# MoE expert weights of a two-block transformer kernel: one transfer per expert with both halves of a row, in place of one transfer per half over all eight experts

## The chip, the cores and the metric

The kernel runs on one core of a Trainium2 chip. The metric is the device time of one execution in microseconds (us), lower is better. The core has a matrix engine (PE, with its weight loads PEld), a vector engine (DVE), a scalar engine (ACT), a sync engine (SP, here the only one that issues transfers) and 16 DMA engines that move data from HBM into on-chip memory.

## The reference

Two transformer blocks in float32 on 256 tokens of width 1024. The change touches one stage of the first block, a mixture of experts: each token is processed by two of eight experts, whose weights are the largest arrays of the program.

```
D_MODEL = 1024; SEQ = 256; N_EXPERTS = 8; TOP_K = 2; FFN_EXPERT = 3584
...
top_logits, top_idx = lax.top_k(logits, TOP_K)
gates = jax.nn.softmax(top_logits, axis=-1)
...
def expert_block(args):
    xb, e = args
    h = jax.nn.silu(xb @ w1[e]) * (xb @ w3[e])     # w1, w3: 1024 x 3584 for each expert
    return h @ w2[e]                               # w2: 3584 x 1024 for each expert
```

Around it stand, in this order, two mixer layers (gated delta rule, convolution, attention), a dense SwiGLU between them, and, after the experts, a second block with two attention layers and two gated feed-forward layers. None of these is touched.

## The kernel before

**Storage.** The host lays the expert weights out as `ws_moe`: for each of the 8 experts 42 slots, and a slot is 128 rows (one for each partition) of 2048 floats, so a row is 8 KB, a slot 1 MB, and the same slot of the next expert lies 42 slots (44 MB) further on. In the first 28 slots of an expert a row holds for one column block of 128 the w1 weights of all eight input blocks and then the w3 weights of the same (4 KB each: the two "halves", h = 0 and 1). In the last 14 slots a row holds weights of w2.

**Chunks.** The stage runs over 84 chunks (`CHUNKS`), each of 4 MB: 4 input blocks (`CK = 4`) of 128 x 256 weights for all eight experts. 56 chunks belong to the up phases (w1 and w3), 28 to the down phases (w2). Chunks are loaded in turn into two buffers, `mring[0]` (traced as ring) and `mring[1]` (traced as arena), whose order in a partition is expert, half, 512 floats. Two chunks, one in each buffer, are called a cycle below.

**Who waits for what.** SP issues the loads of chunk c once `chunk_over(c - 2)` holds (L385-392, called at L444): PE has done the products that read chunk c - 2 directly, and DVE and ACT have copied out of it what the dynamic row blocks need. In before each chunk is two transfers (L452), one for each half, and both count up `moe_w0` or `moe_w1`. PE (L904), ACT (L1337) and DVE (L1848) start on a chunk when all of its transfers have landed. DVE then copies with L1860 and ACT with L1351 the weights of the experts that own the dynamic row blocks into small buffers (`CB`, three in turn), and PE multiplies at L913: for each of a chunk's four input blocks 24 row blocks of 32 rows, of which the first eight read the chunk itself and the others the copies. L1833 and L1838/L1840 take the sums out of the accumulators, L894 transposes hidden rows.

**Streams outside the stage.** All other weights come through L416 (`slot_dma`) as 1 MB tiles whose 128 rows of 8 KB are contiguous in HBM.

Of the kernel before, what the change touches and what calls it, by code (L numbers as in the profile page):

```python
# [7 lines left out]
P = 128  # L8
# [9 lines left out]
KD = D // P  # L18
# [6 lines left out]
NE = 8  # L25
FE = 3584
KE = FE // P
# [6 lines left out]
SLOT = 16  # L34
# [10 lines left out]
PK = 4  # L45
NPART = KE // PK
CK = 4
# [60 lines left out]
PHASES = moe_phases()  # L108
PH_CHUNKS = [KD // CK if i < PK else PK // CK for _, i in PHASES]
CHUNKS = [(ph, st) for ph, n in enumerate(PH_CHUNKS) for st in range(n)]  # L110
# [10 lines left out]
def up_index(ph):  # L121

    part, i = PHASES[ph]
    return PK * part + i


def flips_first(c):
# [32 lines left out]
def build(nc, ws_a, ws_moe, ws_b, xT, ctxT, cT, pvec, prow, wsmall, wrouter, cst_d, out):  # L160
    with ExitStack() as ctx:
        sems = {}

        def sem(name):
            if name not in sems:
                sems[name] = ctx.enter_context(nc.semaphore(name))
            return sems[name]
# [157 lines left out]
        SELT = arena_at(17408, NG * T).rearrange("p (g t) -> p g t", g=NG)  # L325
        IOTA2 = arena_at(18944, NROW)
        ws_up = ws_moe.rearrange("(e s) p (w c) -> s w p e c", e=NE, w=2)
        ws_dn = ws_moe.rearrange("(e s) p c -> s p e c", e=NE)
        HT = Mf[:, 0:5 * NROW].rearrange("p (q r) -> p q r", q=5)

# [82 lines left out]
        @block.sync  # L413
        def _(sp):
            def slot_dma(pos, src):
                return sp.dma_start(ring[:, pos * SLOT * P:(pos + 1) * SLOT * P], src)  # L416

            def stream(n):
                if n >= RING:

                    name, count = FREE[n - RING]
                    sp.wait_ge(sem(name), count)
                array, i = SOURCE[n]
                slot_dma(n % RING, (ws_a if array == "a" else ws_b)[i]).then_inc(sem(f"weights{n % RING}"), 16)

            sp.dma_start(X[:, 1], xT).then_inc(sem("x_in"), 16)
            sp.dma_start(cst[:, :], cst_d).then_inc(sem("consts_in"), 16)
            sp.dma_start(pv[:, :], pvec).then_inc(sem("params_in"), 16)
            sp.dma_start(pr[:, :, :], prow).then_inc(sem("rows_in"), 16)
            sp.dma_start(wsm[:, :, :, :], wsmall).then_inc(sem("small_in"), 16)  # L430
            sp.dma_start(wrt[:, :, :], wrouter).then_inc(sem("router_in"), 16)
            sp.dma_start(cvec[:, :, :], cT).then_inc(sem("c_in"), 16)
            for n in range(SLOT0["moe"]):
                stream(n)
            sp.wait_ge(sem("tile_done"), TILE["out1"] + 8)
            sp.wait_ge(sem("ada_done"), 16)
            for c in range(NCH):
                ph, st = CHUNKS[c]
                part, i = PHASES[ph]
                if c == 1:  # L440
                    sp.wait_ge(sem("x_even"), 12)
                    sp.wait_ge(sem("x_odd"), 12)
                if c >= 2:
                    chunk_over(sp, c - 2)  # L444
                to = mring[c % 2].rearrange("p (e h c) -> p e h c", e=NE, h=2)
                for h in range(2):
                    if i < PK:
                        src = ws_up[up_index(ph), h, :, :, st * CK * P:(st + 1) * CK * P]
                    else:
                        t = (2 * (i - PK) + h) * KE + PK * part  # L450
                        src = ws_dn[2 * KE * KD // SLOT + t // SLOT, :, :, t % SLOT * P:(t % SLOT + CK) * P]
                    sp.dma_start(to[:, :, h], src).then_inc(sem(f"moe_w{c % 2}"), 16)  # L452

            for n in range(SLOT0["moe"], len(SOURCE)):
                i = n - SLOT0["moe"]
                if i < RING:
                    if n % RING < 4:
                        chunk_over(sp, NCH - 2)
                    else:
                        unit_over(sp, (CK * NCH - 1) // 3 * 3)  # L460
                    slot_dma(n % RING, ws_b[SOURCE[n][1]]).then_inc(sem(f"weights{n % RING}"), 16)
                    if i == RING - 1:
                        sp.wait_ge(sem("combined"), KD)
                        sp.dma_start(X[:, 0], ctxT).then_inc(sem("ctx_in"), 16)
                else:
                    stream(n)
            for t in range(TT):
                sp.wait_ge(sem("out_ready"), t + 1)
                sp.dma_start(out[t * P:(t + 1) * P, :], Yf[:, t * D:(t + 1) * D]).then_inc(sem("stored"), 16)
            sp.wait_ge(sem("stored"), 16 * TT)  # L470
# [3 lines left out]
        def _(pe):  # L474
# [169 lines left out]
            for l in range(2):  # L644
# [140 lines left out]
                for g in range(G):  # L785
                    r = g % 2 * HD
                    for i in range(2):
                        c = i * HD
# [60 lines left out]
                else:  # L849
# [48 lines left out]
                    for c in range(NCH):  # L898
# [2 lines left out]
                        last = ends_phase(c)  # L901
                        if flips_first(c):
                            flip(up_index(ph - 1))
                        pe.wait_ge(sem(f"moe_w{c % 2}"), 32 * (c // 2 + 1))  # L904
                        if i >= PK:
                            pe.wait_ge(sem("hidden_stored"), 2 * PK * (part + 1))

# [171 lines left out]
        def _(act):  # L1079
# [80 lines left out]
            for l in range(2):  # L1160
# [143 lines left out]
                else:  # L1304
# [27 lines left out]
                    for c in range(NCH):  # L1332
                        ph, st = CHUNKS[c]
                        ended = ends_phase(c - 1) and PHASES[ph - 1][1] < PK
                        if ended:
                            silu(ph - 1, 0)
                        act.wait_ge(sem(f"moe_w{c % 2}"), 32 * (c // 2 + 1))  # L1337
                        for kk in range(CK):
                            u = CK * c + kk
                            if kk == 2 and ended:  # L1340
# [119 lines left out]
        def _(dve):  # L1460
# [82 lines left out]
            for l in range(2):  # L1543
# [217 lines left out]
                else:  # L1761
# [81 lines left out]
                    for c in range(NCH):  # L1843
                        ph, st = CHUNKS[c]
                        ended = ends_phase(c - 1)
                        if ended:
                            take_rows(ph - 1, 0)
                        dve.wait_ge(sem(f"moe_w{c % 2}"), 32 * (c // 2 + 1))  # L1848
                        for kk in range(CK):
                            u = CK * c + kk  # L1850
                            if kk == 2 and ended:
# [316 lines left out]
```

## Time and profile before

| | us |
|---|---|
| median of 3 runs (3202.76 to 3207.5) | 3204.41 |
| the profiled execution, own time | 3191.41 |
| its span | 3189.6 |
| transfers from `ws_moe` | 168 of 2 MB, 352 MB in all |
| PE busy | 2887.9 (91% of the span) |
| DVE busy | 1565.4 (49%) |
| ACT busy | 1042.2 (33%) |

The page gives averages over stages with different limits, so it is read by stage. The expert stage fills about a third of the span, from some 770 us (first loads) and 855 us (both buffers cycling) to some 1920 us. In the page's slices it is the stretch in which the DMA digit stands at 9. A row of the windows view gives for a stretch the busy time of each engine, the granted clock of PE, the busy share of the 16 DMA engines and the GB/s moved. A row of the chain view gives start, length and what the end of the program waited for at that moment.

### The profile page before, as it was taken

The page shows a single profiled execution, that of the slowest core. Times are in us where ns is not written, and L with a number is a line of the kernel's source. Part 1 is how long each engine was busy: PE and PEld are TensorE (multiplying, and loading weights), DVE is VectorE, ACT ScalarE, POOL GpSimd, SP SyncE. Part 2 cuts the span into 40 slices and gives each one's busy share as a digit, 9 for nine tenths or more (in the row PEclk, how much of TensorE's full clock was granted, in tenths as well). Part 3 has the DMA queues.
Part 4 walks back from the last instruction along what each step waited for, and adds up shares of the span by engine and source line. Part 5 has one row for each costly group of instructions (what it writes and reads, how often), then busy time and mean ns, then how long its engine had stood idle before and what let it go on. Part 6 is the DMA issues. An engine that isn't in the chain of part 4 may idle for free.

```text
span 3189.6 us, 67930 instructions
## 1 busy us (share of the span) xinstructions
PE 2887.9 (91%) x26308; PEld 1876.5 (59%) x26308; DVE 1565.4 (49%) x5142; ACT 1042.2 (33%) x2749; POOL 0.2 (0%) x4
## 2 busy tenths in 40 slices
PE   8979999978888888888888887989999999899998
PEld 7858887856455555555555545444444444556887
DVE  5641005563567676777676673784322210454331
ACT  3121002221455545554555552253211100243210
POOL 0000000000000000000000000000000000000000
PEclk9979999988999999999999998999999999999999
DMA  5444434454599999999999981100121221211441
GB/s 206 167 172 171 146 133 158 151 207 159 191 327 322 326 321 325 327 327 315 329 318 330 322 306 65 58 26 27 66 77 69 79 79 66 79 54 54 154 150 66
DMA packets 205858, 576.06 MB, mean 181 GB/s; under 512 B 6496, under 2 KB 6624, under 8 KB 179040
## 3 DMA queue, kind: packets, MB, share of 16 engines
q1 hardware_dynamic: 205536, 571.72, 52.0%
q8 instruction: 208, 3.41, 0.4%
q14 instruction: 114, 0.93, 0.1%
HBM read 570.65 MB, written 1.05 MB: 179 GB/s over the span
## 4 chain that ended last, share of the span: by engine, by line
PE 60%; DMA 21%; DVE 13%; issue 3%; ACT 2%; DVEq 1%; SPq 1%; ACTq 0%
PE P L497 43%; DMA ring<-ws_moe 20%; PE P L913 4%; DVE arena L1860 4%; DVE ring L1860 2%; PE P L686 1%; PE P L544 1%; PE P L608 1%; DVE small L1518 1%; PE P L618 1%; DVEq L1857 1%; PE P L627 1%; PE P L881 1%; PE P L576 1%; PE P L958 1%
## 5 line engine op out<-in xcount | busy, mean ns | idle before, releaser
L497 PE MATMUL P<-arena,ring 128*128 128x256 f32 (+1 forms) x2784 | 900.2, 484 | 24.7 <-ACT arena L1157 24.7
L497 PEld LDWEIGHTS P<-arena,ring 128*128 128x128 f32 x2784 | 531.9, 192 | 383.0 <-issue 335.4
L913 PE MATMUL P<-arena 128*32 128x256 f32 x6496 | 368.4, 379 | 12.1 <-DVE rstd L1833 6.6
L913 PE MATMUL P<-ring,arena 128*32 128x256 f32 x4256 | 279.3, 414 | 80.0 <-DMA ring<-ws_moe 71.2
L497 PE MATMUL P<-X_sb,ring 128*128 128x256 f32 x1504 | 333.7, 383 | 2.9 <-ACT X_sb L1136 1.6
L497 PEld LDWEIGHTS P<-X_sb,ring 128*128 128x128 f32 x1504 | 286.6, 192 | 45.1 <-issue 3.1
L1860 DVE COPY arena<-ring 128x256 f32 x1120 | 234.6, 290 | 146.8 <-DMA ring<-ws_moe 134.6
L913 PEld LDWEIGHTS P<-arena 128*32 128x32 f32 x6496 | 213.3, 110 | 150.4 <-DVE ring L1860 9.1
L1860 DVE COPY arena<-arena 128x256 f32 x1120 | 233.7, 290 | 74.1 <-DMA arena<-ws_moe 63.3
L913 PEld LDWEIGHTS P<-ring,arena 128*32 128x32 f32 x4256 | 148.3, 119 | 196.5 <-DMA ring<-ws_moe 83.7
L1351 ACT ACTIVATE arena<-ring 128x256 f32 x560 | 181.5, 405 | 222.5 <-DMA ring<-ws_moe 163.6
L1351 ACT ACTIVATE arena<-arena 128x256 f32 x560 | 180.9, 405 | 120.7 <-PE P L913 60.5
L913 PE MATMUL P<-arena,MIX 128*32 128x256 f32 x3360 | 192.0, 379 | 14.9 <-DVE Y L1838 7.5
L2004 DVE SCALAR_TENSOR_TENSOR arena<-P,pv,arena 128x510 f32<-128x510 f32 (+1 forms) x88 | 54.2, 616 | 290.0 <-ACT arena L1399 201.4
L1916 DVE SCALAR_TENSOR_TENSOR X_sb<-P,mod,X_sb 128x256 f32<-128x256 f32 x48 | 23.2, 484 | 296.7 <-PE P L497 296.1
L913 PEld LDWEIGHTS P<-arena,MIX 128*32 128x32 f32 x3360 | 119.2, 110 | 80.6 <-DVE arena L1860 13.3
L913 PE MATMUL P<-ring,MIX 128*32 128x256 f32 x2016 | 127.5, 401 | 37.9 <-DMA ring<-ws_moe 25.0
L1860 DVE COPY ring<-ring 128x256 f32 x560 | 118.4, 290 | 65.4 <-DMA ring<-ws_moe 57.5
L497 PE MATMUL P<-MIX,ring 128*128 128x256 f32 (+1 forms) x512 | 145.7, 441 | 2.2 <-issue 2.2
L1860 DVE COPY ring<-arena 128x256 f32 x560 | 118.3, 289 | 39.6 <-DMA arena<-ws_moe 35.0
L1351 ACT ACTIVATE ring<-ring 128x256 f32 x280 | 91.8, 406 | 104.7 <-DMA ring<-ws_moe 70.2
L497 PEld LDWEIGHTS P<-MIX,ring 128*128 128x128 f32 x512 | 99.4, 195 | 44.1 <-issue 33.5
(360 smaller groups left out, 2564.7 us busy)
## 6 DMA issues: line engine op xcount, KB each, us to landing
ring<-ws_moe SPq DMA_DIRECT2D x84, 2048.0 KB, 13.8
arena<-ws_moe SPq DMA_DIRECT2D x84, 2048.0 KB, 15.5
ring<-ws_b SPq DMA_DIRECT2D x137, 1024.0 KB, 4.8
ring<-ws_a SPq DMA_DIRECT2D x67, 1024.0 KB, 4.9
cst_sb<-cst SPq DMA_DIRECT2D x1, 1664.0 KB, 8.5
X_sb<-xT SPq DMA_DIRECT2D x1, 1024.0 KB, 4.8
X_sb<-ctxT SPq DMA_DIRECT2D x1, 1024.0 KB, 4.9
out<-Y SPq DMA_DIRECT2D x2, 512.0 KB, 2.6
```

The lines of the kernel that those rows point to most:

```text
L497: ins = nc.tensor.matmul(bank(i, n), blockap(s, b % SLOT), rhs(kk), start=kk == 0, stop=kk == k - 1)
L544: ins = nc.tensor.matmul(P0[32 * j:32 * j + 32, b, 256 * half:256 * half + 256], csil[:, k, :], w, start=k == 0, stop=k == KD - 1)
L576: ins = nc.tensor.matmul(P1[:, 0, 0:n], c_("ones"), SQH[:, k, 0:n], start=k == 0, stop=k == KD - 1)
L608: nc.tensor.matmul(P1[:, (2 * p + i) % 4, 0:nk * P], q, kk, start=True, stop=True)\
L618: ins = nc.tensor.matmul(P0[i * HD:(i + 1) * HD, p % 2, 0:P], vfn(h + i, j), ptb[:, (2 * p + i) % 4, j * P:(j + 1) * P], start=j == 0, sto ...
L627: ins = nc.tensor.transpose(P0[:, 2 + i, j * P:(j + 1) * P], pb[:, (2 * p + i) % 6, j * P:(j + 1) * P], c_("ident"))
L686: ins = nc.tensor.matmul(P1[c:c + HD, 2 * i + h, r * HD:(r + 1) * HD], lhs[c:c + HD, g], cident[c:c + HD] if rhs is None else rhs[c:c + HD ...
L881: ins = nc.tensor.matmul(acc8(n % 8)[:, 0:w], XTM[:, t, k * P:(k + 1) * P], SEL[:, t, at:at + w], start=t == 0, stop=t == TT - 1)
L913: ins = nc.tensor.matmul(acc(g // 2)[BR * j:BR * (j + 1), g % 2], x[:, b * BR:(b + 1) * BR], weights_of(b), start=k == 0, stop=last and kk ...
L1351: ins = a.activation(CB[u % 3][:, NDVE + j].rearrange("p (h c) -> p h c", h=2), src, ACT.Copy)
L1860: ins = v.tensor_copy(CB[u % 3][:, j].rearrange("p (h c) -> p h c", h=2), src)
L2004: L(v.scalar_tensor_tensor(f3[:, :, 1:], b3[:, :, 0:T - 1], pv[:, w0 + 3 * m:w0 + 3 * m + 1], f3[:, :, 1:], ALU.mult, ALU.add))
```

## The change

A chunk of an up phase becomes eight transfers, one for each expert: 128 rows, and of each row two pieces of 2 KB that lie 4 KB apart (w1's and w3's). A chunk of a down phase becomes sixteen transfers, one for each expert and half: 128 rows with one piece of 2 KB. The pieces, their number and their places in the buffers are as before; the waits of PE, ACT and DVE count the new number of transfers (`landed`). The waits of SP are as before, ahead of the first transfer of a chunk.

```diff
+def landed(c):
+    return sum(16 * NE * (1 if PHASES[CHUNKS[n][0]][1] < PK else 2) for n in range(c % 2, c + 1, 2))
...
         ws_up = ws_moe.rearrange("(e s) p (w c) -> s w p e c", e=NE, w=2)
+        ws_row = ws_moe.rearrange("(e s) p (w c) -> e s p w c", e=NE, w=2)
         ws_dn = ws_moe.rearrange("(e s) p c -> s p e c", e=NE)
...
                 to = mring[c % 2].rearrange("p (e h c) -> p e h c", e=NE, h=2)
-                for h in range(2):
+                for e in range(NE):
                     if i < PK:
-                        src = ws_up[up_index(ph), h, :, :, st * CK * P:(st + 1) * CK * P]
-                    else:
+                        sp.dma_start(to[:, e], ws_row[e, up_index(ph), :, :, st * CK * P:(st + 1) * CK * P])\
+                            .then_inc(sem(f"moe_w{c % 2}"), 16)
+                        continue
+                    for h in range(2):
                         t = (2 * (i - PK) + h) * KE + PK * part
-                        src = ws_dn[2 * KE * KD // SLOT + t // SLOT, :, :, t % SLOT * P:(t % SLOT + CK) * P]
-                    sp.dma_start(to[:, :, h], src).then_inc(sem(f"moe_w{c % 2}"), 16)
+                        sp.dma_start(to[:, e, h], ws_dn[2 * KE * KD // SLOT + t // SLOT, :, e, t % SLOT * P:(t % SLOT + CK) * P])\
+                            .then_inc(sem(f"moe_w{c % 2}"), 16)
...
-                        pe.wait_ge(sem(f"moe_w{c % 2}"), 32 * (c // 2 + 1))
+                        pe.wait_ge(sem(f"moe_w{c % 2}"), landed(c))
```

The order of transfers on SP before, from the second pair of chunks of the first up phases on to the first down chunks (shape: partitions x experts x floats):

```order
43 L452 DMA ring<-ws_moe 128x8x512 [waits copied_act,copied_dve,fixed_done]
44 L452 DMA ring<-ws_moe 128x8x512
45 L452 DMA arena<-ws_moe 128x8x512 [waits copied_act,copied_dve,rows_done]
46 L452 DMA arena<-ws_moe 128x8x512
47 L452 DMA ring<-ws_moe 128x8x512 [waits copied_act,copied_dve,fixed_done]
48 L452 DMA ring<-ws_moe 128x8x512
49 L452 DMA arena<-ws_moe 128x8x512 [waits copied_act,copied_dve,rows_done]
50 L452 DMA arena<-ws_moe 128x8x512
```

The same place on SP with the change (L454: an up chunk, partitions x halves x floats; L459: a down chunk, partitions x floats):

```order
43 L454 DMA ring<-ws_moe 128x2x512 [waits copied_act,copied_dve,fixed_done]
44 L454 DMA ring<-ws_moe 128x2x512 x7
45 L454 DMA arena<-ws_moe 128x2x512 [waits copied_act,copied_dve,rows_done]
46 L454 DMA arena<-ws_moe 128x2x512 x7
47 L459 DMA ring<-ws_moe 128x512 [waits copied_act,copied_dve,fixed_done]
48 L459 DMA ring<-ws_moe 128x512 x15
49 L459 DMA arena<-ws_moe 128x512 [waits copied_act,copied_dve,rows_done]
50 L459 DMA arena<-ws_moe 128x512 x15
```

No row has moved against another: where two transfers stood behind a wait, eight or sixteen stand there now. The other engines' rows are as before.

## Rows read from the trace of the kernel before

**Rows 1.** The page's slices of 80 us: DMA share in tenths, GB/s.

```profile
DMA  5444434454599999999999981100121221211441
GB/s 206 167 172 171 146 133 158 151 207 159 191 327 322 326 321 325 327 327 315 329 318 330 322 306 65 58 26 27 66 77 69 79 79 66 79 54 54 154 150 66
```

**Rows 2.** Windows view, 1000 us of the expert stage.

```profile
core 0: us, PE busy (x) PEld busy (x) DVE busy (x) ACT busy (x) POOL busy (x), PEclk, DMA share, GB/s
863.00:1863.00 1000.00, 866.77 (x14872) 519.51 (x14864) 697.22 (x3205) 528.74 (x1656) 0.00 (x0) 0.96 0.98 324
```

**Rows 3.** Windows view of the same stretch, instructions of L913 alone.

```profile
863.00:1863.00 1000.00, 847.67 (x14716) 502.96 (x14708) 0.96 0.98 324
```

**Rows 4.** DMA view of the same stretch: packets, queue's share of 16 engines, issues to landing.

```profile
DMA packets 159741, 324.30 MB, mean 324 GB/s; under 512 B 2458, under 2 KB 2458, under 8 KB 159545
q1 hardware_dynamic: 159545, 321.72, 96.9%
arena<-ws_moe SPq DMA_DIRECT2D x78, 2048.0 KB, 14.0
ring<-ws_moe SPq DMA_DIRECT2D x76, 2048.0 KB, 13.8
```

**Rows 5.** Chain of waits, 850:1960, first and last of 39 alike; the stretch's shares.

```profile
by line: DMA ring<-ws_moe 56.9%; PE P L913 11.7%; DVE arena L1860 11.0%; DVE ring L1860 5.6%; issue 4.8%; DVEq L1857 2.7%; PE P L958 1.9%; SPq L452 1.3%; DVE X_sb L1838 0.6%; DVE Y L1838 0.4%; PE P L531 0.3%; PE P L522 0.3%; DVE MIX L1485 0
...
855.86 15.74 DMA ring<-ws_moe
...
1846.96 15.96 DMA ring<-ws_moe
```

**Rows 6.** Chain of waits, one cycle of it (start, length, what).

```profile
1011.90 0.37 SPq L452
1012.27 0.04 issue
1012.31 16.04 DMA ring<-ws_moe
1028.35 0.04 issue
1028.40 7.01 PE P L913 x96
...
1036.79 0.89 DVE arena L1860 x4
1037.73 0.37 SPq L452
1038.14 16.34 DMA ring<-ws_moe
```

**Rows 7.** Timeline of SP: when the chunks' loads are issued.

```profile
1011.90 0.99 SPq L452 DMA_DIRECT2D ring<-ws_moe  x2
1023.46 0.99 SPq L452 DMA_DIRECT2D arena<-ws_moe  x2
1037.73 1.47 SPq L452 DMA_DIRECT2D ring<-ws_moe  x2
1049.02 1.60 SPq L452 DMA_DIRECT2D arena<-ws_moe  x2
```

**Rows 8.** Timeline of ACT, the first work on a landed arena chunk.

```profile
1039.85 1.64 ACT L1351 ACTIVATE arena<-arena 128x256 f32 x5 [1.38 <-DMA arena<-ws_moe]
```

**Rows 9.** DMA view, 1026:1052, GB/s in 40 slices of 0.65 us.

```profile
GB/s 249 391 378 394 400 403 394 388 375 366 388 378 328 287 334 337 369 359 296 139 255 268 306 290 299 331 359 321 296 252 293 337 290 262 353 321 388 321 299 170
```

**Rows 10.** Windows view: parts of one cycle, then streams of 1 MB tiles (columns as Rows 2).

```profile
1026.50:1034.00 7.50, 5.60 (x76) 2.90 (x80) 5.50 (x26) 5.25 (x17) 0.00 (x0) 0.77 1.04 383
1039.50:1052.00 12.50, 12.33 (x232) 7.15 (x220) 8.60 (x41) 6.62 (x21) 0.00 (x0) 1.00 1.00 303
...
134.00:139.00 5.00, 4.94 (x133) 3.96 (x130) 4.72 (x9) 0.98 (x2) 0.00 (x0) 1.00 1.00 415
133.50:139.50 6.00, 5.94 (x168) 4.96 (x166) 5.57 (x10) 0.98 (x2) 0.00 (x0) 1.00 1.02 425
```

**Rows 11.** Chain of waits at the stage's end, where PE is not kept waiting.

```profile
1869.74 16.53 PE P L913 x288
...
1895.69 22.34 PE P L913 x384
```

**Rows 12.** Timeline of SP at the program's start: small and large transfers issued in a row.

```profile
1.17 0.42 SPq L427 DMA_DIRECT2D cst_sb<-cst  x1
1.65 0.42 SPq L428 DMA_DIRECT2D pv<-pvec  x1
2.11 0.67 SPq L429 DMA_DIRECT2D pr<-prow  x1
2.83 0.44 SPq L430 DMA_DIRECT2D wsm<-wsmall  x1
3.31 0.49 SPq L431 DMA_DIRECT2D wrt<-wrouter  x1
```

**Rows 13.** Waits of DVE, ACT and PE on chunks and on each other, 863:1863.

```profile
ACT arena L1351 <- DMA ring<-ws_moe: 146.1, 25, 7.4
DVE arena L1860 <- DMA ring<-ws_moe: 125.1, 25, 6.7
PE P L913 <- DMA ring<-ws_moe: 92.7, 37, 4.2
PE P L913 <- DMA arena<-ws_moe: 5.8, 5, 2.3
```

More of the change, by code:

```diff
@@ L1336, in _ @@
                             silu(ph - 1, 0)
-                        act.wait_ge(sem(f"moe_w{c % 2}"), 32 * (c // 2 + 1))
+                        act.wait_ge(sem(f"moe_w{c % 2}"), landed(c))
                         for kk in range(CK):
@@ L1847, in _ @@
                             take_rows(ph - 1, 0)
-                        dve.wait_ge(sem(f"moe_w{c % 2}"), 32 * (c // 2 + 1))
+                        dve.wait_ge(sem(f"moe_w{c % 2}"), landed(c))
                         for kk in range(CK):
```

## The prediction

> **What bounds the kernel now.** I read the page's slices first, to find the stage that the change touches and what is full there. In twelve slices of 80 us the DMA digit is 9 and the traffic 315 to 330 GB/s, nowhere else [rows 1]. A window of 1000 us inside that stage shows the 16 DMA engines 98% busy at 324 GB/s, and PE 866.77 us busy at a clock of 0.96 [rows 2]. So this stage is bound by the transfers; everything outside it has DMA to spare and isn't touched by the change, so the whole effect must come out of the stage.
>
> Next the chain of waits. Between 855.86 and 1846.96 it passes 39 times through a load of the ring buffer, so 38 cycles of two chunks take 991.1 us, **26.08 us a cycle** [rows 5]. One cycle reads: load of ring 16.04 us, 7.01 us of products on it, some 2.3 us of copies, SP's issue 0.37 us, and the load again [rows 6]. The load of a 4 MB chunk is issued when the other chunk's is nearly in: ring's at 1037.73 [rows 7], the arena chunk before it starts ACT at 1039.85 [rows 8], 2.1 us later. So two things agree within a few tenths: the transfers of a cycle (8.39 MB), and the loop of load, products, copies and issue. Both shrink only if bytes come faster. PE waits 92.7 us for ring and 5.8 us for arena chunks in the 1000 us [rows 13].
>
> How fast do bytes come when the queue is full? 321.72 MB at a share of 96.9% of 1000 us are 332 GB/s while busy, or, for 2 KB pieces (157,000 in that time, with the small packets that end a transfer taken off), 16 x 969 us / 157,000 = **98.7 ns a piece and engine** [rows 4]. At that rate a cycle's 8.39 MB take 25.27 us; the other 0.81 us of the 26.08 is the queue running dry when ring's load is issued late, the dip to 139 GB/s in a cycle's slices [rows 9].
>
> **The change, part by part.**
>
> *The same bytes, asked for in another order.* This is the part that can pay. Before, the pieces that one engine reads one after the other come from eight experts, 44 MB apart; with the change they come from one expert's slot, 4 KB or 8 KB apart. No row of this trace shows that order with pieces of 2 KB. The bounds are these. From below, what 2 KB pieces get today: 332 GB/s on average, and 303 GB/s in the worse part of a cycle [rows 10]. From above, 8 KB rows of one contiguous slot, which the 1 MB tiles reach with three transfers queued: 415 to 425 GB/s [rows 10]. Between them lies what 2 KB pieces get in the better part of a cycle, 383 GB/s over 7.5 us, with slices to 403 [rows 9, 10]. That last row matters most: it is the same pieces into the same buffers, so neither their size nor the write side forces 332, and something that comes and goes (I take it to be collisions in HBM) costs the difference. It does not prove that the order is the cause. A loss of rate is not excluded either: in the new order all 16 engines read inside one slot at the same time, and if they collide there, the rate falls; 303 GB/s is the nearest row for that. I take **360 GB/s**, midway between today's 332 and the 383 to 403 of the good stretches with some weight on their lower end, nearer to 2 KB rows than to the 8 KB rows, since a piece stays 2 KB. Then a cycle's bytes take 8.39 / 360 = 23.3 us.
>
> Here a rule of the Trainium skill bears on the sum (DMA: Bandwidth & Descriptors, section Latency and other measured facts, on HBM row pitch at large powers of two): copies whose rows lay 2 MiB apart fell to 164 GB/s and those at 4 MiB to 103, and it takes channel collisions as the likely cause. Our experts' pitch is 42 MiB, a multiple of 2 MiB. This trace's 324 GB/s shows that the loss in full isn't there, since the rows of a partition run are 8 KB apart and only the inner step is wide; by the rule's direction the sum would come out at the 8 KB rows' rate, that is the PE rival below.
>
> *More transfers.* 56 chunks x 8 + 28 x 16 = 896 in place of 168: 21.3 a cycle in place of 4, so 17.3 more. Each ends in one small packet on each engine (2458 packets under 512 B for 154 transfers, 16 each) [rows 4]. Three queued 1 MB tiles, which hand over every eight rows an engine, keep 425 GB/s over 6 us, and 415 over the 5 us inside it [rows 10]; if all of that difference of 2.4% were the price of the handover it would be 0.06 us each 2.5 us. So a handover costs 0 to 0.06 us, 0 to 1.04 us a cycle. I take 0.1 us a cycle, near the low end, because the window with more handovers isn't the slower one.
>
> A second rule of the skill speaks against the change (the same page, Rules for kernel authors): at least 1 MiB for each transfer, and its formula of about 2 us fixed would make 2.6 us of each 256 KB. If that were paid in series the stage would double. The trace disagrees for queued transfers: the tiles above move at 425 GB/s with several in flight, which leaves no 2 us between them.
>
> *SP's issue.* One issue takes 0.42 to 0.67 us, one each 0.48 us or so, and hardly depends on size [rows 12]; today's pairs take 0.99 to 1.60 us [rows 7]. Eight take 3.8 us, sixteen 7.7 us. A 512 KB transfer drains in 1.6 us and one of 256 KB in 0.8 us at 324 GB/s, both slower than 0.48, so SP stays ahead of the engines, and 7.7 us end before SP's next release, 11.6 to 14.3 us later [rows 7]. Nothing else is queued on SP in the stage. Cost nothing. Without that cover (an issue of over 0.8 us) the down chunks would be issue-bound.
>
> *The waits.* PE, ACT and DVE still start on a chunk when all of it is in, and SP still waits for the same events; no chunk starts earlier in its own load. The count in the wait costs nothing.
>
> *The sum.* By the transfers: 23.3 + 0.8 (dry queue) + 0.1 = 24.2 us a cycle. By the loop: ring's load is 16.3 us now, of which 4.19 MB at 303 GB/s are 13.8; with that scaled by 360/332 to 12.8 it is 15.3, and with the 9.7 us of products, copies and issue 25.0; but the 2.1 us for which it stands behind arena's rest shrink as the transfers get ahead, down to some 1 us of start, which gives 24.0. I take **24.3**. The gain is 26.08 - 24.3 = 1.78 us, x 38 = 68 us. The profiled execution took 3191.4 us and would take 3124; the median of the runs lies 13 us higher, so 3204.4 - 68 = **3137 us**. What comes next to the transfers is PE: a cycle's 384 products take 22.34 us where nothing makes them wait [rows 11], and the transposes add (866.77 - 847.67) / 38.3 = 0.5 us [rows 2, 3], so 22.8 us.
>
> **The rivals.**
>
> *PE becomes the bound.* If the new order reaches 400 GB/s or more, the bytes take 21 us and PE's 22.8 us set the cycle: 3.2 x 38 = 123 us, **3081 us**. For it: the contiguous tiles' 415 to 425 GB/s. Against it: the loop must also close, and pieces remain 2 KB.
>
> *The rate stays.* The slow pieces may come from another cause (bursts after a dry queue, refresh, other traffic), which the order doesn't touch. Then only the 0.1 us of handovers is left: + 4 us, **3208 us**. For it: the rate swings between 303 and 383 GB/s inside one cycle with one and the same order [rows 10].
>
> *Handovers, slower.* In the stage each engine gets only eight or sixteen pieces a transfer, 0.8 to 1.6 us of work, where the tiles have 2.5 us. If closing one and taking up the next costs 0.1 us, 17.3 a cycle are 1.7 us, x 38 = 66 us, **3270 us**; at 0.06 us, the upper bound above, + 39 us, 3244 us. With today's rate it makes the kernel slower by over 0.2% from 10 ns a handover on; against the gain that I forecast it would need over 0.11 us. For it: nothing in the trace shows transfers so small in a row. Against it: the stream of tiles at 425 GB/s. The skill's rule on 1 MiB stands on this side.
>
> **How the numbers follow.** Forecast 3137 (its own range 3095 to 3190): 0.55. PE bound, 3081: 0.07. Rate stays, 3208: 0.14. Slower by handovers or by collisions inside one slot, 3225 to 3290: 0.24. A measurement of this kernel can tell about 0.2% (6.4 us) from no change. Faster 0.62, same 0.14, slower 0.24. The range 3080 to 3245 takes in the PE bound and handovers up to 0.06 us, and leaves out the upper half of the slower case and a little below.
>
> **What would show it.** In the changed profile: GB/s of 340 to 370 in the slices of the stage with the DMA share still 9; ring loads on the chain every 24.3 us; PE busy share in the stage up from 87% to 93%, PE's wait for ring down from 93 us in 1000 to about half; issues to landing near 14 us for the last transfer of a chunk. GB/s at 400 or PE at 98% would show the PE rival, 324 GB/s at share 98% the unchanged rate, and a share that falls below 95% or GB/s below 310 the handovers. The forecast is wrong if HBM's order has no say, or if small transfers leave gaps.

## The result: slower by 0.6%, with the transfers no faster and more of them

| | before | after |
|---|---|---|
| median of 5 runs (lowest to highest; before: with the three already given), us | 3204.41 (3200.19 to 3207.5) | 3223.39 (3220.51 to 3228.07) |
| ratio after / before | | 1.0059 (95% interval 1.0046 to 1.0073) |
| profiled execution, span | 3189.6 | 3221.0 |

The forecast was 3137 us, 68 us faster; the kernel became 19 us slower. The spans of the two profiled executions differ by more, 31.4 us: the profile of before (own time 3191.41 us) is not one of its five runs here and is 9 us faster than the fastest of them, while on the other chips the kernel before had medians of 3189 to 3194 us. So of what the two traces differ by, some 12 us are not the change's. Where the two traces are compared below, the direction is the change's and the size is too large.

The page of after, slices of 80 us (DMA share in tenths, GB/s), and its packets, answer to [rows 1]:

```profile
DMA  5444444444799999999999982100122212211441
GB/s 208 164 176 163 157 144 143 146 196 157 232 300 311 320 316 317 314 321 315 307 313 326 318 296 93 66 27 20 60 79 78 79 61 83 73 58 53 145 153 68
DMA packets 217511, 576.15 MB, mean 179 GB/s; under 512 B 18144, under 2 KB 18272, under 8 KB 190688
...
PE 60%; DMA 14%; DVE 12%; SPq 8%; issue 3%; ACT 2%; DVEq 1%; ACTq 0%
```

The same shares of the chain before:

```profile
PE 60%; DMA 21%; DVE 13%; issue 3%; ACT 2%; DVEq 1%; SPq 1%; ACTq 0%
```

The stage moves 300 to 326 GB/s where it moved 315 to 330, and the small packets that end a transfer have grown from 6496 to 18144, which is 16 for each of 728 further transfers. In the shares of the chain SP's issue of transfers (SPq) has grown from 1% to 8% of the whole span, and the transfers themselves have shrunk from 21% to 14%.

The same 1000 us as [rows 2] and [rows 4], windows view and DMA view of after:

```profile
863.00:1863.00 1000.00, 850.49 (x14422) 501.01 (x14414) 677.53 (x3111) 512.39 (x1606) 0.00 (x0) 0.95 0.95 315
DMA packets 165436, 315.18 MB, mean 315 GB/s; under 512 B 12611, under 2 KB 12611, under 8 KB 165241
q1 hardware_dynamic: 165241, 312.64, 93.8%
```

Two readings decide the case. **While busy** the queue moves 312.64 MB / 938 us = 333 GB/s; it was 332. With the new order and number together the rate stayed where it was. **The busy share** fell from 96.9% to 93.8%: the engines stand idle 6.2% of the time in place of 3.1%, that is 1.67 us of a cycle of 26.85 us in place of 0.81 us of one of 26.08. The difference of 0.86 us, 33 us over 38 cycles, fits the 31.4 us between the two traces; the change's own part by the medians is 19 us, 0.5 us a cycle.

SP's timeline of after (answers to [rows 7]; x8: the eight transfers of an up chunk, x16 of a down chunk):

```profile
932.07 11.65 SPq L459 DMA_DIRECT2D ring<-ws_moe  x16
943.83 9.88 SPq L459 DMA_DIRECT2D arena<-ws_moe  x16
...
1017.65 5.60 SPq L454 DMA_DIRECT2D ring<-ws_moe  x8
1027.77 8.47 SPq L454 DMA_DIRECT2D arena<-ws_moe  x8
1044.36 5.68 SPq L454 DMA_DIRECT2D ring<-ws_moe  x8
1056.09 6.61 SPq L454 DMA_DIRECT2D arena<-ws_moe  x8
1071.34 5.85 SPq L454 DMA_DIRECT2D ring<-ws_moe  x8
```

Ring loads are issued at 1017.65, 1044.36 and 1071.34: cycles of 26.85 us. Over the stage from 852 us on, issuing a chunk takes 5.4 to 9.1 us for eight and 8.2 to 11.7 us for sixteen, not the 3.8 and 7.7 of the forecast. At 943.72 SP ends the sixteenth issue and begins the next chunk at 943.83, so there it may have come late for a release; that is the only place in the cycling part of the stage with a gap of half a microsecond or less. Elsewhere SP is done earlier, by 5.6 us in the median over all chunks.

### The profile page after: what moved, and what is told of

It reads as the page before. It is cut to its first block, busy times and chain, and to the rows that moved or that the text cites. A ratio compares the mean times of both kernels' runs of the same rounds, so it can differ in the third digit from the quotient of the medians.

```text
span 3221.0 us, 68658 instructions
## 1 busy us (share of the span) xinstructions
PE 2897.2 (90%) x26308; PEld 1873.5 (58%) x26308; DVE 1565.3 (49%) x5142; ACT 1041.5 (32%) x2749; POOL 0.2 (0%) x4
## 2 busy tenths in 40 slices
DMA packets 217511, 576.15 MB, mean 179 GB/s; under 512 B 18144, under 2 KB 18272, under 8 KB 190688
## 4 chain that ended last, share of the span: by engine, by line
PE 60%; DMA 14%; DVE 12%; SPq 8%; issue 3%; ACT 2%; DVEq 1%; ACTq 0%
PE P L505 43%; DMA ring<-ws_moe 10%; PE P L921 5%; SPq L454 4%; SPq L459 4%; DVE arena L1868 3%; DMA arena<-ws_moe 3%; DVE ring L1868 2%; PE P L694 1%; PE P L552 1%; PE P L616 1%; DVE small L1526 1%; PE P L626 1%; DVEq L1865 1%; PE P L635 1%
## 5 line engine op out<-in xcount | busy, mean ns | idle before, releaser
L921 PE MATMUL P<-arena 128*32 128x256 f32 x6496 | 377.2, 385 | 24.2 <-DMA arena<-ws_moe 14.0
```

The source lines that it names most:

```text
L921: ins = nc.tensor.matmul(acc(g // 2)[BR * j:BR * (j + 1), g % 2], x[:, b * BR:(b + 1) * BR], weights_of(b), start=k == 0, stop=last and kk ...
```

## The experiments

Theory A: each further transfer costs the 16 engines idle time. Theory B: the changed order, one expert's slot at a time, reads slower. Theory C: the order helps, and the number costs more than it brings. Later, two pairs of theories refine these. By A1 the cost lies at each handover from one transfer to the next; by A2 it lies in SP's issue after the queue ran dry. By P the rate suffers from rows at a pitch of 8 KB of which only fixed 2 KB pieces are read; by J it suffers from the jumps of 44 MB. A ratio is to the kernel before on the same chip, with its 95% interval.

### One part of the change alone

Up chunks per expert, down chunks as before:

```diff
+                if i < PK:
+                    for e in range(NE):
+                        sp.dma_start(to[:, e], ws_row[e, up_index(ph), :, :, ...]) ...
+                else:
...
```

> Only the up chunks are loaded as eight transfers, one for each expert with both halves of a row; the down chunks stay at two transfers. 336 of the 728 further transfers remain. Theory A (each further transfer costs the 16 engines some idle time, whatever the order of pieces): 336/728 of the measured +19 us, so +9 us, ratio 1.0027, and the DMA share of the stage about midway between 98% and 95%. Theory B (reading one expert's slot with all 16 engines at once is slower than reading eight slots in turn; the number is harmless): both kinds of chunk read one slot at a time in the changed kernel, so the share by bytes, 56/84 of 19 us = +13 us, ratio 1.0040. Theory C (the order helps and the number costs more than the sum shows): the up chunks have the smaller number for each byte and all of the adjacent halves, so near 0 or a gain.

Measured: 3202.99 against 3192.94 us, ratio **1.0035 (1.0023 to 1.0047)**.

Down chunks in sixteen, up chunks as before:

```diff
                         src = ws_dn[2 * KE * KD // SLOT + t // SLOT, :, :, t % SLOT * P:(t % SLOT + CK) * P]
-                    sp.dma_start(to[:, :, h], src) ...
+                    for e in range(NE):
+                        sp.dma_start(to[:, e, h], src[:, e]) ...
```

> Only the down chunks are cut into sixteen transfers, one for each expert and half; the up chunks stay at two. 392 of the 728 further transfers remain. Theory A (number): 392/728 of +19 us = +10 us, ratio 1.0032. Theory B (one slot at a time is slower): 28/84 of 19 us = +6 us, ratio 1.0020. Theory C (order helps, number costs more): more than +10 us, ratio over 1.004.

Measured: 3198.24 against 3192.94 us, ratio **1.0013 (1.0003 to 1.0024)**. Together 1.0048, the change within its interval. Both parts lose, so neither shows a gain, and theory C has no support. Between A (1.0027, 1.0032) and B (1.0040, 1.0020) these two lean to B: A's 1.0032 lies outside the second interval, so a further transfer doesn't cost the same in both kinds of chunk (30 ns against 13). B isn't shown by that. The DMA views of the two, the same 1000 us, say more than the times:

```profile
q1 hardware_dynamic: 163008, 318.70, 95.6%
...
q1 hardware_dynamic: 163951, 319.49, 96.0%
```

First the up chunks alone, then the down chunks: 333 GB/s while busy in both, as before, and busy shares of 95.6 and 96.0% between 96.9 and 93.8. In these two the rate didn't move; the idle time did.

### The number without the change's order

The order of before, halves then experts, cut into transfers of two experts, eight a chunk:

```diff
+                    for e in range(0, NE, 2):
+                        sp.dma_start(to[:, e:e + 2, h], src[:, e:e + 2]) ...
```

> The order of before (a half at a time, experts in turn), cut into transfers of two experts: eight transfers a chunk, for up and down alike, 504 further transfers, and of the pieces that an engine reads one after the other every second is still 44 MB away. Theory A (number): 504/728 of +19 us = +13 us, ratio 1.0041, stage share near 95.5%. Theory B (order): within 3 us of the kernel before, ratio 1.000 to 1.001.

Measured: 3203.36 us, ratio **1.0029 (1.0014 to 1.0043)**, busy share 94.5%, 336 GB/s while busy. With pieces that still alternate between two experts 44 MB apart, about half of the change's loss is there, 10.4 us for 504 of its 728 transfers; theory A had said 13. Theory B in its pure form (1.000 to 1.001) falls.

Cut down to one expert and half, sixteen for every chunk (`range(0, NE, 1)` in the same diff):

> The order of before cut to the smallest transfers, one expert and one half each: sixteen a chunk, for up and down alike, 1176 further transfers. The runs so far show 44 to 53 ns of idle engine time for each further 512 KB transfer and 26 ns for each further 256 KB one, with the rate while busy unchanged at 333 to 336 GB/s. Theory A (number, some 26 ns for one of 256 KB): 1176 x 26 ns = +31 us, ratio 1.010. Theory B (order): as before, 1.000 to 1.001.

Measured: 3220.41 against 3194.18 us, ratio **1.0078 (1.006 to 1.0096)**: 26 us for 1176 further transfers, 22 ns each, a little under the forecast 26. The loss grows in proportion to the number: 10 us for 504 transfers (21 ns each), 26 us for 1176. By these two, which keep the order of before, the 728 of the change would cost 15 to 16 us; the other 3 to 4 of the 19 lie within the change's interval, so a small price of the order is neither shown nor excluded. Part of this run's loss can be SP's: at 1078.77, 1347.29 and 1720.68 us it ends the sixteenth issue of a chunk, and begins the next chunk only 0.11 to 0.12 us later.

### Where the cost of a transfer lies

One half cut into eight transfers of 256 KB, the other left whole (the diff shows the cut of the first half, h = 0; the mirror run has h == 1 there):

```diff
+                    n = 1 if h == 0 else NE
+                    for e in range(0, NE, n):
+                        sp.dma_start(to[:, e:e + n, h], src[:, e:e + n]) ...
```

> The order of before; of each chunk the first half is cut into eight transfers of 256 KB, the second stays one of 2 MB: nine a chunk, 588 further transfers, all at the start of a chunk, where the queue has run dry or nearly so. Theory A1 (each handover costs the engines a gap wherever it lies): +15 us, ratio 1.005, the same as with the small transfers at the end of a chunk. Theory A2 (the cost is SP's issue: after the queue ran dry the engines are fed one small transfer each half microsecond or so): all of it here, +15 to +25 us, ratio 1.005 to 1.008.

> The mirror of the run with the small transfers first: of each chunk the first half is one transfer of 2 MB and the second eight of 256 KB. Theory A1 (a gap at each handover): +15 us, ratio 1.005. Theory A2 (SP's issue after a dry queue): 2 MB are queued before the first small one, so nothing is left of the cost, ratio 1.000 to 1.001.

Measured: small ones first **1.0041 (1.0028 to 1.0055)**, small ones last **1.0039 (1.0028 to 1.005)**: 12.1 and 13.8 us of the medians for 588 further transfers, 21 and 23 ns each. Theory A2 (only behind a dry queue) said 1.000 to 1.001 for the second. It falls: a cut costs the same, within the noise, with 2 MB queued ahead of it.

Nothing cut, but four transfers of 16 x 8 bytes behind each of the two of 2 MB:

```diff
                     sp.dma_start(to[:, :, h], src) ...
+                    for j in range(4):
+                        sp.dma_start(spare[0:16, c % 2, h, j, :], pvec[0:16, 0:2]).then_inc(sem(f"moe_w{c % 2}"), 16)
```

> The kernel before with four transfers of 16 x 8 bytes behind each 2 MB transfer: ten a chunk, 672 further transfers which bring no data of use and one piece of 8 bytes for each engine. It prices a transfer by itself, without the pieces of the chunk being cut. Theory A1 (a gap at each handover, some 26 to 50 ns): 17 to 34 us, ratio 1.005 to 1.011. Theory A2 (SP's issue after a dry queue): the first 2 MB of each chunk go out as before, so the second 2 MB wait behind four issues of 0.45 us while 6 us of data are queued: 1.000 to 1.001, or 2 us for the small packets themselves.

Measured: 3233.41 us, ratio **1.0115 (1.0098 to 1.0133)**, 39 us for 672 transfers, 58 ns each, a little above the range of A1. Here the order of the chunk's pieces is exactly that of before, so more transfers cost time without any change of order. The price is not that of a cut: a tiny transfer brings two small packets on each engine, its 8 bytes and the one that ends it (21246 under 512 B in the 1000 us), where a cut brings one. And the engines wait for the tiny ones too: 38.7% of the chain from 840 to 1960 us are their transfers. SP's timeline shows that their issue is held up:

```profile
1016.75 0.39 SPq L458 DMA_DIRECT2D ring<-ws_moe  x1
1017.18 2.73 SPq L460 DMA_DIRECT2D spare<-pvec  x4
1019.96 0.42 SPq L458 DMA_DIRECT2D ring<-ws_moe  x1
1020.42 4.70 SPq L460 DMA_DIRECT2D spare<-pvec  x4
1027.42 0.39 SPq L458 DMA_DIRECT2D arena<-ws_moe  x1
1027.85 3.36 SPq L460 DMA_DIRECT2D spare<-pvec  x4
1031.26 0.45 SPq L458 DMA_DIRECT2D arena<-ws_moe  x1
1031.75 6.24 SPq L460 DMA_DIRECT2D spare<-pvec  x4
```

Four issues of 0.45 us would take 1.8; they take 2.7 to 6.2. What in a handover costs 13 to 58 ns the records don't tell, and I leave it open.

Nor is the loss all idle time. The DMA views of 863:1863, first sixteen to a chunk, then the tiny ones:

```profile
q1 hardware_dynamic: 172167, 313.50, 95.5%
...
q1 hardware_dynamic: 172699, 310.30, 95.0%
```

The sixteen leave the engines busier than the eight of two experts did (95.5% against 94.5%), and yet cost more, since the rate while busy is 328 GB/s where the eight had 336; the tiny ones have 327. The small packets count as busy time. So the busy share alone doesn't price the number of transfers; the time does.

### What the rate depends on

Pieces of 4 KB: the host lays the two halves of a chunk side by side in each row, two transfers of four experts each (s and w are the slot and the half of its rows that hold the chunk).

```diff
-    up = np.stack([w1, w3], axis=1).transpose(0, 4, 3, 1, 2, 5).reshape(NE, KE, P, SLOT * P)
+    up = np.stack([w1, w3], axis=1).reshape(NE, 2, KD // CK, CK, P, KE, P).transpose(0, 5, 4, 2, 1, 3, 6)...
...
+                src = ws_dn[s, :, :, w * 8 * P:(w + 1) * 8 * P]
+                for e in range(0, NE, 4):
+                    sp.dma_start(to[:, e:e + 4].rearrange("p e h c -> p e (h c)"), src[:, e:e + 4]) ...
```

> The host lays each row out so that the two halves of a chunk stand side by side, for up and down alike: pieces of 4 KB in place of 2 KB, half as many; two transfers a chunk of four experts each, experts in turn as in before. It measures what the size of a piece is worth against its order. If the slow pieces of before are collisions by address (my forecast's mechanism), each 4 KB piece still comes from another expert, 44 MB on, and the collisions stay, though half as many: a gain of 10 to 30 us. If the 2 KB size is what costs, the rate goes from 332 toward the 415 to 425 GB/s of 8 KB rows, the cycle of two chunks falls from 26.1 to PE's 22.8 to 24 us: 80 to 120 us faster, ratio 0.963 to 0.975. If neither, 0.

Measured: 3084.88 against 3192.94 us, ratio **0.9666 (0.9649 to 0.9683)**, 108 us faster. The DMA view of 863:1763 and what PE waited for there (of before, after it: the same waits):

```profile
q1 hardware_dynamic: 81099, 322.10, 92.0%
...
PE P L920 <- DVE rstd L1840: 27.7, 26, 1.3
PE P L920 <- DVE Y L1845: 17.2, 15, 1.3
PE P L920 <- DMA ring<-ws_moe: 9.3, 12, 1.3
```

```profile
PE P L913 <- DMA ring<-ws_moe: 87.4, 35, 4.2
PE P L913 <- DVE Y L1838: 11.6, 10, 1.5
PE P L913 <- DVE rstd L1833: 11.1, 10, 1.3
```

322.10 MB / (0.920 x 900 us) = 389 GB/s while busy, with every piece still 44 MB from the one before it. So the far jump doesn't forbid a high rate. The 108 us are what was expected if the size of a piece counts. PE's wait for ring chunks has shrunk from 87.4 to 9.3 us.

Then the addresses alone. Transfers and pieces of before (two transfers, 2 KB, experts in turn), but the host lays the eight experts' pieces of a half chunk side by side, 16 KB in a row:

```diff
-                        src = ws_up[up_index(ph), h, :, :, st * CK * P:(st + 1) * CK * P]
...
+                near = ws_moe.rearrange("(n a) p c -> n (a p c)", a=2).rearrange("n (p e c) -> n p e c", p=P, e=NE)
+                n = 2 * (2 * up_index(ph) + st) if i < PK else 4 * KE + 2 * (PK * part + i - PK)
+                for h in range(2):
+                    sp.dma_start(to[:, :, h], near[n + h]) ...
```

> The transfers and pieces of before (two transfers a chunk, pieces of 2 KB, experts in turn), only their addresses differ: the host lays the eight experts' pieces of a half chunk side by side, so that an engine reads 16 KB in a row where it jumped 44 MB after each 2 KB. The order of addresses alone. If far jumps cost the rate (the mechanism of my forecast): the rate while busy rises from 332 to 360 GB/s or more and the time falls by 60 us or more, ratio under 0.982. If the size of a piece is what costs (4 KB pieces 44 MB apart came at 389 GB/s): rate near 332, ratio 0.997 to 1.002.

Measured: 3120.64 against 3189.0 us, ratio **0.9785 (0.9765 to 0.9805)**, 68 us faster. DMA view, 863:1763:

```profile
DMA packets 154515, 313.70 MB, mean 349 GB/s; under 512 B 2369, under 2 KB 2369, under 8 KB 154326
q1 hardware_dynamic: 154326, 311.22, 96.4%
```

The packets are as many for their bytes as in [rows 4], so the pieces are still 2 KB; the rate while busy is 311.22 / (0.964 x 900) = 359 GB/s, and a piece takes 16 x 867.6 us / 151,957 = 91.4 ns and engine where it took 98.7. Size isn't all: addresses matter. This layout removed two things at once, the far jumps and the holes: in before and after alike a chunk reads 2 KB and leaves out 2 KB, in rows 8 KB apart.

Padding tells them apart. It leaves transfers, pieces, jumps and holes alone and moves the rows from 8 to 10 KB apart, so that a chunk's pieces fall on even and odd multiples of 2 KB in turn; once for the kernel before, once for the changed one:

```diff
+        ws_moe = ws_moe[:, :, 0:SLOT * P]
...
+    ws_moe = np.concatenate([ws_moe, np.zeros((NE * MOE_SLOTS, P, 4 * P), np.float32)], axis=2)
```

> The kernel before; the host pads each 8 KB row of the expert weights by 2 KB, so that rows stand 10 KB apart and the pieces of one chunk fall on even and odd multiples of 2 KB in turn, over all addresses. Transfers, pieces and the far jumps between experts are as in before (52.5 MiB where it was 42). Theory P (a chunk that touches only every second 2 KB at a pitch of 8 KB uses the memory unevenly): the rate rises from 332 toward the 359 GB/s of the adjacent pieces, 50 to 70 us faster, ratio 0.978 to 0.985. Theory J (the far jumps, or the break after each 2 KB, cost): ratio 0.998 to 1.002.

> The changed kernel with the same padding of rows to 10 KB. Theory P: the rate rises here too, and the changed kernel keeps only its loss by the number of transfers: 19 us slower than the padded kernel before, 30 to 50 us faster than the kernel before, ratio 0.985 to 0.991. Theory J with the jump as the cost: nothing changes, ratio 1.004 to 1.008, as without padding.

Measured: before padded 3102.98 against 3191.94 us, ratio **0.9718 (0.9699 to 0.9737)**; the changed kernel padded 3123.47 us, **0.9784 (0.9764 to 0.9805)**. DMA views of 863:1763, before padded, then the changed kernel padded:

```profile
DMA packets 156992, 318.72 MB, mean 354 GB/s; under 512 B 2416, under 2 KB 2416, under 8 KB 156799
q1 hardware_dynamic: 156799, 316.19, 97.4%
...
DMA packets 163938, 312.25 MB, mean 347 GB/s; under 512 B 12526, under 2 KB 12526, under 8 KB 163745
q1 hardware_dynamic: 163745, 309.75, 96.5%
```

361 and 357 GB/s while busy. Theory P holds, and gives more than it said: 89 us where 50 to 70 were expected, and 68 us where 30 to 50 were. The jumps are not what costs: the changed kernel has none inside a transfer, had 333 GB/s without padding, and its rate rises like the other's with it. (Padding moves the experts' pitch from 42 to 52.5 MiB too; for the kernel before alone that would leave a doubt, the changed kernel removes it.) And between the padded two the same 728 transfers cost 20.5 us again, 28 ns each, as 19 us without padding. So the price of the number remains when that of the addresses is gone.

### The cut in faster layouts

The 4 KB pieces with one transfer for each expert (`range(0, NE, 1)` in the 4 KB diff):

> Pieces of 4 KB (the two halves side by side by the host's layout), one transfer for each expert: eight a chunk, the cut of the changed kernel in the faster layout, 504 transfers more than the 4 KB run with two a chunk. If a handover costs some 21 to 26 ns of the engines' time but the stage is no longer bound by them: within 4 us of that run, ratio 0.966 to 0.968. If the loop still passes through the load: +10 to +13 us, ratio 0.970.

Measured: 3119.13 us, ratio **0.978 (0.9758 to 0.9802)**, against 0.9666 with two transfers. Both expectations were too low: the cut costs 1.1% here. As the loss is 34 us for 504 transfers, 68 ns each, it is more than the number cost with 2 KB pieces. To see whether its holes (4 KB read, 4 KB left out) have a part, eight transfers that are contiguous blocks of 512 KB:

```diff
+                blocks = ws_moe.rearrange("(n a) p c -> n (a p c)", a=4).rearrange("n (e p c) -> n e p c", e=NE, p=P)
+                n = 2 * up_index(ph) + st if i < PK else 2 * KE + PK * part + i - PK
+                for e in range(NE):
+                    sp.dma_start(mring[c % 2][:, 1024 * e:1024 * (e + 1)], blocks[n, e]) ...
```

> Eight transfers a chunk, one for each expert, each a block of 512 KB that is contiguous in HBM (128 rows of 4 KB, no holes): number, size and pieces of the 4 KB run with eight transfers (ratio 0.978), but without its holes. The 4 KB run with two transfers had 0.967, the contiguous chunk with two 0.960. If the number of transfers made the loss of 0.978: 0.974 to 0.980 again. If the order of half-used rows of one slot made it: 0.960 to 0.968.

Measured: 3097.46 us, ratio **0.9707 (0.9688 to 0.9726)**: between the two expectations. DMA views of 863:1763, eight transfers with holes, then without:

```profile
q1 hardware_dynamic: 85289, 310.57, 94.2%
...
q1 hardware_dynamic: 87003, 316.81, 93.3%
```

These are 366 and 377 GB/s while busy, where two transfers of four experts with holes had 389. Of the 1.1% some 0.7 are gone without the holes. How it divides isn't shown: a run with two transfers of 4 KB pieces without holes is missing, so it stays open whether the order of one half-used slot at a time costs something here or the holes cost the two-transfer run as well. With 4 KB pieces the rate while busy fell with the cut by 6%, more than in any run with 2 KB pieces.

### The version that beats both

The whole chunk side by side in HBM, two transfers of 128 rows of 16 KB:

```diff
+                rows = ws_moe.rearrange("(n a) p c -> n (a p c)", a=4).rearrange("n (p c) -> n p c", p=P)
+                n = 2 * up_index(ph) + st if i < PK else 2 * KE + PK * part + i - PK
+                for h in range(2):
+                    sp.dma_start(mring[c % 2][:, 4096 * h:4096 * (h + 1)], rows[n, :, 4096 * h:4096 * (h + 1)]) ...
```

> The host lays a whole chunk side by side; two transfers a chunk of 128 rows of 16 KB, contiguous in HBM and in the buffer. Against the run with 4 KB pieces (3.3% faster than before). The transfers should come at 415 to 425 GB/s while busy. If PE's 22.8 us a cycle bind now, that brings little more: 0.3 us a cycle, 10 us, ratio 0.962 to 0.968. If the loop of load, products and copies still binds, the shorter load gives 1 us a cycle: ratio 0.955.

Measured: 3062.45 against 3189.0 us, ratio **0.9604 (0.9583 to 0.9624)**, 127 us faster. DMA view and PE's waits, 863:1763, and the first and last of 39 ring loads on its chain:

```profile
q1 hardware_dynamic: 22551, 328.59, 90.9%
...
PE P L916 <- DVE rstd L1836: 22.1, 26, 1.1
PE P L916 <- DMA ring<-ws_moe: 4.6, 8, 1.0
```

```profile
849.96 13.23 DMA ring<-ws_moe
...
1717.24 13.01 DMA ring<-ws_moe
```

402 GB/s while busy, under the 415 to 425 that was expected, the engines idle a tenth of the time, and 867.28 / 38 = 22.8 us a cycle. The ratio lies between the two expectations. The forecast's bound by PE was 22.8 us as well, but the trace doesn't show that PE binds. Its windows row for 863:1763, and its chain over one cycle (where the dots stand there are only DVE's entries, nearly all of them copies):

```profile
863.00:1763.00 900.00, 849.09 (x15154) 537.16 (x15144) 717.37 (x3287) 543.08 (x1702) 0.00 (x0) 1.00 0.92 368
```

```profile
1009.20 12.95 DMA ring<-ws_moe
1022.29 0.09 DVE ring L1863
...
1030.26 0.88 DVE ring L1863 x4
1031.20 0.33 SPq L454
1031.57 13.14 DMA ring<-ws_moe
```

PE is busy 94% of the time at a granted clock of 1.00 (the 2.4 GHz level), 21.5 us of a cycle. The chain passes through ring's load (13 us), 9.05 us of DVE's copies and SP's issue, and through no product. So here the loop of load and copies sets the cycle, and PE has 1.3 us of it to spare.

## Why the prediction was wrong, point by point

**What bounds the stage** was right. Every run that made the transfers faster or slower moved the time with them, down to the contiguous chunk, where the queue is idle 9% of the time.

**The rate, 360 GB/s: this step failed**, and it carried the whole gain. The trace had shown that 2 KB pieces can do better (383 GB/s in part of a cycle), and I put that down to collisions in HBM that a nearer order would avoid. The addresses do count: the padding alone brings 361 GB/s. That these are collisions in HBM no run shows. But I took it that nearer is better, and didn't ask which property of the addresses the change leaves as it is. It leaves both that count: the rows stand 8 KB apart and of each 4 KB only one and the same 2 KB is read. What it removed, jumps of 44 MB, costs nothing that can be seen: 333 GB/s against 332. Why the rate swings between 303 and 383 GB/s inside one cycle was not looked into.

The page of the Trainium skill that I named (DMA: Bandwidth & Descriptors, section Latency and other measured facts) says of the row pitch, for pitches from 512 KiB up, that padding by a few KiB restores the rate. The runs agree in kind at a pitch of 8 KB: 2 KB of padding gave 2.8% of the kernel's time. I had applied it to the experts' pitch, and it lay with the rows' pitch.

**From the rate to the time: right in the main.** I worked out a cycle of 24.3 us and 68 us of gain for 360 GB/s. The run with adjacent pieces had 359 GB/s and was 68 us faster. That it agrees to the microsecond is luck: the padded kernel before had 361 GB/s and was 89 us faster, with its engines busy 97.4% of the time where the run with adjacent pieces had 96.4%. On the chain of the run with adjacent pieces 39 loads of ring stand between

```profile
854.88 14.58 DMA ring<-ws_moe
...
1777.24 14.31 DMA ring<-ws_moe
```

so 922.36 / 38 = 24.3 us a cycle.

**The handovers: right in kind, mis-sized.** I bounded a handover at 0 to 60 ns and took 6 ns, since streams of 1 MB tiles showed no price. Measured were 13 to 30 ns for a cut of the 2 KB pieces and 58 ns for a tiny transfer. At the 21 to 28 ns of the pairs, the singles and the padded kernels the 728 of the change are 15 to 20 us, so most or all of the 19 us. In place of the term of 0.1 us a cycle stands one of 0.4 to 0.5. The row that I leaned on has a handover every 2.5 us, and 26 ns of that is 1%, less than the two windows that I compared differ by; it could not have shown the price. The low end was a choice without a row.

**SP's issue: too short.** The small transfers at the program's start were no measure for these: 5.4 to 11.7 us a chunk in place of 3.8 and 7.7. (The shortest time to the next release in [rows 7] is 11.3 us, not 11.6.) It did no harm that the runs show by itself, since small transfers cost the same at a chunk's end as at its start, but for chunks of sixteen the cover is thin.

**The rivals.** The one that the rate stays had the effect of the order right, at 3208 us. The third rival said that with today's rate handovers above 10 ns make the kernel slower; at the 21 to 28 ns of the runs that gives 3204 + 15 to 20 us, and 3223 was measured. I had priced the third at 60 to 100 ns, so the truth lay between the two, and the likeliest case was the wrong one. The sign that I had named for the handovers, a busy share below 95%, came: 93.8% of the queue. **PE's bound**, 22.8 us a cycle, looks confirmed by the contiguous chunk, which had that cycle and was 127 us faster than its own before, where 123 was forecast for the bound. But that is luck in part. The 22.34 us of [rows 11] for 384 products were taken at a granted clock of 0.93; in the contiguous run, at 1.00, 384 products take 828.44 / 14992 x 384 = 21.2 us (L916 in 863:1763), and the loop of load and copies held the cycle at 22.8.

**What stays open.** Why the pitch counts, in the memory or elsewhere, is not shown; the runs show only that moving the pitch by 2 KB, or leaving no holes, brings 2 KB pieces to 357 to 361 GB/s. What happens in the 13 to 58 ns of a handover isn't in the records.

## What to carry to other kernels

When a stage is bound by its transfers, divide the bytes by the busy share first: it splits a slow queue into a low rate while busy (here pieces and addresses) and idle engines (here late issue and part of the price of many transfers), and a change can only mend what it touches. The split isn't clean for many small transfers, so price their number by a run that changes nothing else. If a transfer reads short pieces at a power of two pitch (8 KB here, the only one tried) and leaves holes at fixed places, try padding the rows or laying the pieces side by side before another order; the host does it outside the measured time, and padding costs a quarter more memory. Don't cut a queue of large transfers into small ones unless something can start on a part of the data.

## What the runs showed of the hardware

- 2 KB pieces: 327 to 336 GB/s while busy at a row pitch of 8 KB, in each order of experts and number of transfers that was run, 357 to 361 GB/s at 10 KB, 359 GB/s side by side. 4 KB pieces at 8 KB pitch: 389 GB/s with experts in turn, 366 GB/s with a transfer for each expert, 377 GB/s as contiguous blocks. Rows of 16 KB: 402 GB/s.
- A further queued transfer costs the kernel 13 to 30 ns when it comes from cutting a larger one (2 KB pieces), at the head of a chunk's load (21 ns) as at its tail (23 ns), and 58 ns when it is a tiny one added.
- Tiny transfers can hold their issuer longer than large ones: four of 16 x 8 bytes kept SP 2.7 to 6.2 us, where two of 2 MB in the kernel before kept it 0.99 to 1.60 us.
- PE's products ran at a granted clock of 0.95 to 0.96 in the stage while it waited for loads (before and after), and of 1.00 in the 4 KB, adjacent and contiguous runs.
